# Which pieces of weights go through the fifth slot: new lists for mixers and FFNs of a two-block transformer forward pass

## What is computed

```
for l in range(2):                                   # first block
    x = x + 0.5 * swiglu(rmsnorm(x), w_ffn1_in[l], w_ffn1_out[l])      # 1024 -> 2*2816 -> 1024
    u = rmsnorm(x); parts = split(u @ w_in[l])
    y = mla_branch (8 heads, causal), hgrn2_branch (4 heads, gated recurrence, chunks of 64),
        memory_branch (4 heads over 256 memory tokens)
    x = x + (sum of sigmoid(gate_i) * (y_i @ w_o_i)) @ w_out[l]
    x = x + 0.5 * swiglu(rmsnorm(x), w_ffn2_in[l], w_ffn2_out[l])
x = rmsnorm(x)
for l in range(2):                                   # second block
    FFN, then x = x + concat(rwkv7_group, retnet_group) @ w_out_2[l], then FFN
return rmsnorm(x)
```

## Time and profile before

| | us |
|---|---|
| three runs | 2357.98, 2355.84, 2358.05; median 2357.98 |
| the profiled execution's own time | 2355.99 |
| its span, first to last instruction | 2354.2 |
| PE busy | 2333.3 (99%) |
| DVE busy | 1639.6 (70%) |
| ACT busy | 1277.4 (54%) |
| DMA queue q1 | 401.62 MB, 47.4% of 16 engines |

### The profile page before, as it was taken

How to read it: one execution, slowest core, us unless ns; L and a number is a source line. 1 busy time by engine, 2 the same in 40 slices (tenths; PEclk the granted TensorE clock), 3 DMA queues, 4 the chain that set the end, 5 groups by cost and what they waited for, 6 DMA issues and landing times.

```text
span 2354.2 us, 50733 instructions
## 1 busy us (share of the span) xinstructions
PE 2333.3 (99%) x21750; PEld 2275.3 (97%) x21750; DVE 1639.6 (70%) x2270; ACT 1277.4 (54%) x1828; POOL 346.9 (15%) x296
## 2 busy tenths in 40 slices
PE   9999999999999999999999999999999999999998
PEld 9999999999999999999999999989999999989998
DVE  7865777966677657878666766776765766776763
ACT  6644656654455456565455554636554554646554
POOL 2012020300200210203003002431002002431001
PEclk9999999999999999999999999999999999999999
DMA  6555533465555545335555645422655545422643
GB/s 255 202 193 194 179 126 126 180 213 182 197 194 190 192 180 185 118 141 183 197 196 181 223 180 197 168 80 91 215 180 197 197 182 196 173 74 92 216 180 124
DMA packets 57680, 410.21 MB, mean 174 GB/s; under 512 B 6384, under 2 KB 6640, under 8 KB 8688
## 3 DMA queue, kind: packets, MB, share of 16 engines
q1 hardware_dynamic: 56448, 401.62, 47.4%
q10 hardware_dynamic: 1008, 5.34, 0.6%
HBM read 405.89 MB, written 1.05 MB: 173 GB/s over the span
## 4 chain that ended last, share of the span: by engine, by line
PE 84%; DVE 7%; ACT 4%; issue 4%; POOL 1%; DMA 0%; DVEq 0%; ACTq 0%; SPq 0%; POOLq 0%
PE bank L558 83%; DVE sb_wlo L514 3%; DVE area L1862 1%; ACT sb_whi L506 1%; PE bank L2210 1%; ACT area L1582 0%; DVE area L1845 0%; DVE area L1811 0%; DVE area L648 0%; POOL sb_x_ssq L701 0%; ACT area L1648 0%; DVE area L1919 0%; ACT area L1606 0%; POOL area L839 0%; ACT area L1603 0%
## 5 line engine op out<-in xcount | busy, mean ns | idle before, releaser
L558 PE MATMUL bank<-area,sb_whi 128*128 128x256 f32 x11752 | 2017.1, 278 | 3.1 <-ACT area L782 1.2
L558 PEld LDWEIGHTS bank<-area,sb_whi 128*128 128x128 f32 x11752 | 1769.1, 188 | 12.6 <-issue 4.2
L558 PE MATMUL bank<-area,sb_wlo 128*128 128x256 f32 x5876 | 1606.4, 277 | 5.2 <-DVE sb_wlo L514 5.0
L506 ACT ACTIVATE sb_whi<-sb_raw 128x1024 fp32r<-128x1024 f32 x762 | 793.0, 1055 | 596.0 <-PE bank L558 582.6
L558 PEld LDWEIGHTS bank<-area,sb_wlo 128*128 128x128 f32 x5876 | 1094.4, 188 | 7.7 <-DVE sb_wlo L514 7.6
L514 DVE TENSOR_TENSOR sb_wlo<-sb_raw,sb_whi 128x1024 fp32r<-128x1024 f32 x762 | 954.7, 1264 | 156.8 <-ACT sb_whi L506 154.9
L648 DVE TENSOR_TENSOR area<-bank,sb_x_diag 128x512 f32<-128x512 f32 x244 | 166.8, 684 | 72.0 <-PE bank L558 49.7
L999 DVE TENSOR_TENSOR area<-area,area 128x256 f32<-128x256 f32 x176 | 76.2, 433 | 186.7 <-ACT area L950 185.5
L558 PE MATMUL bank<-area,area 64*64 64x64 f32 (+5 forms) x2864 | 149.5, 248 | 0.1
L558 PEld LDWEIGHTS bank<-area,area 64*64 64x64 f32 (+3 forms) x2864 | 127.3, 139 | 19.2 <-ACT area L1630 5.3
L693 POOL TENSOR_TENSOR sb_x_ssq<-sb_x 128x256 f32<-128x256 f32 x9 | 12.0, 1331 | 849.3 <-DVE sb_x L1043 839.1
(11 more groups left out here) (272 smaller groups left out, 1148.3 us busy)
## 6 DMA issues: line engine op xcount, KB each, us to landing
sb_raw<-stream SPq DMA_DIRECT2D x379, 1024.0 KB, 4.8
sb_raw<-stream SPq DMA_DIRECT2D x3, 512.0 KB, 7.2
area<-lora ACTq DMA_DIRECT2D x2, 768.0 KB, 6.1
area<-c ACTq DMA_DIRECT2D x1, 1504.0 KB, 7.5
sb_x<-x SPq DMA_DIRECT2D x4, 256.0 KB, 5.4
area<-mem ACTq DMA_DIRECT2D x1, 1024.0 KB, 8.5
out<-sb_x SPq DMA_DIRECT2D x4, 256.0 KB, 2.9
sb_raw<-stream ACTq DMA_DIRECT2D x1, 512.0 KB, 4.8
```

Of the source, the lines that this page charges most:

```text
L506: e.activation(k.hi[k.slot[p]], raw_piece(k, p), ACT.Copy).then_inc(*k.done("weights_hi", p))
L558: return e.matmul(out, lhsT, rhs, start=start, stop=stop, skip_group_check=True, tile_position=at)
```

## The change

Only the lists differ, and one rule: the same set of pieces used to be at least four apart and now need be only two apart.

```diff
-SEEDS_FIRST, SEEDS, SEEDS_LATE = (0, 4, 18, 40), (2, 23, 45), (0, 4, 25, 47)
-SEEDS_MIX1 = (2, 8, 12, 16, 20, 24, 30, 35, 39, 43, 47, 51, 55, 59, 63, 67, 75)
-SEEDS_MIX2 = (4, 8, 12, 16, 22, 26, 30)
+SEEDS_FIRST, SEEDS, SEEDS_LATE, SEEDS_TWO = (0, 4, 18, 40), (2, 23, 45), (0, 4, 25, 47), (2, 9, 23, 45)
+SEEDS_MIX1 = (2, 8, 24, 30, 33, 39, 41, 43, 45, 47, 49, 51, 53, 55, 59, 61, 63, 67, 75, 78)
+SEEDS_MIX2 = (4, 8, 12, 22, 28)
...
             if i == 0:
                 want = SEEDS_FIRST
+            elif phases[i - 1].endswith("norm"):
+                want = SEEDS_TWO
...
-    assert all(q - p >= SPLIT_SLOTS for p, q in zip(out, out[1:]))
+    assert all(q - p >= 2 for p, q in zip(out, out[1:]))
```

## The result

| | before | after |
|---|---|---|
| median of four runs, us | 2358.02 (2355.84 to 2358.13) | 2420.76 (2419.47 to 2424.45) |
| ratio, 95% interval | | 1.0272 (1.0259 to 1.0285) |
| span of the profiled execution | 2354.2 | 2418.1 |
| sum forecast, over the profiled execution | | +46.9 |
| measured, over the profiled execution | | +63.9 |

The kernel became slower by 62.7 us in the medians. The forecast of 2405.0 was 15.8 short; the range of 2378 to 2426 holds the result.

The account below looks back on a forecast made before the run. PE, busy 99%, seemed the bound, but ACT's splits waiting for PE's seeds would close a loop through ACT and DVE. Costs 50.6 less gains 3.7 make 46.9 over 2355.99, 2402.9; plus 2.0 for the median, 2405 us (range 2378 to 2426).

Parts of the forecast that it names:

- the ring: Attention: PE's seed, ACT's split, ACT's step, DVE's step, PE's next seed wait in a circle; 18.4 us a mixer.
- The tests I had named: Attention: 10 long ACT waits per mixer, seeds 10 to 12 us apart, PE idle before level products, about 25 us longer.
- eight links at the mean of four, 2.3: Attention: eight seeds per mixer each priced at the 2.3 us mean of four worked-out steps, 18.4 us.
- a granted clock of 1.00: Attention: PE's granted clock stays 1.00, 2.4 GHz; the forecast is wrong if it leaves that; no cost counted.
- Rival 4: Attention: PE's clock falls to half while it stands idle, 108 us more over both mixers, about 2510; chance 0.03.
- the end of the attention: Piece 129 waits for 127, delaying ACT's chain that PE needs at piece 130: 4.7 us a mixer.
- the waits of pieces 99 and 127: Piece 99 waits for 96 and 127 for 125: 1.1 us each, the middle of nothing to 2.3.
- The gains: Faster matmuls in B0f1 (1.4), first-block mixers (1.7) and second-block mixers (0.6): 3.7 us saved.
- the two rhythms: PE: the same matmul takes 117.8 ns or 113.3 ns; a seed turns slow into fast, buying 4.4 ns each.
- The first, a hidden wait: Attention: slack behind ACT's split hides the wait, leaving only 3.7 us saved, 2354; chance 0.05.
- The second: Attention: each step costs only as the cheapest of four, 0.7 us, giving 2375; chance 0.05 at its far end.
- third: Attention: each step costs as the dearest of four, 3.9 us, giving 2430; chance 0.05 at its far end.

Follow-up runs that it names:

- the last version: Changed kernel with 33 back to 35, 61 out, ACT's splits running to p + 3 in attention steps 0 to 10: 2352.42 us against 2355.81 for the kernel before.

## Why the prediction was right in sign and short in size

**The ring was right, and so was its arithmetic.** Each sum ran from the end of one seed to the end of the next. The end of a seed is where the next piece starts, or, where ACT waits for it, the start of ACT's split:

| from the end of piece | forecast, us | measured | before | cost |
|---|---|---|---|---|
| 109 to 111 | 12.3 | 12.29 | 8.46 | 3.8 |
| 111 to 113 | 10.7 | 10.63 | 8.53 | 2.1 |
| 117 to 119 | 11.6 | 11.59 | 9.28 | 2.3 |
| 119 to 121 | 10.1 | 10.15 | 8.81 | 1.3 |

ACT's timeline of the changed kernel has the ends of the pieces 113, 117 and 119 (those of 109 and 111 stand above, at 334.70 and 346.99):

```profile
357.62 1.06 ACT L508 ACTIVATE sb_whi<-sb_raw 128x1024 fp32r<-128x1024 f32 x1 [6.33 <-PE bank L560]
...
380.65 1.06 ACT L508 ACTIVATE sb_whi<-sb_raw 128x1024 fp32r<-128x1024 f32 x1 [7.09 <-PE bank L560]
...
392.24 1.06 ACT L508 ACTIVATE sb_whi<-sb_raw 128x1024 fp32r<-128x1024 f32 x1 [7.03 <-PE bank L560]
```

All four sums are within 0.1 us. That the ring is the cause is shown by the kernel with ACT three ahead: same seeds, nothing lost in the steps. The tests I had named were met: waits of 6 to 10 us on ACT, seeds 10 to 12 us apart, PE idle ahead of the level products for DVE.

**The step that failed first: eight links at the mean of four, 2.3.** The eight links of A0mix, with no fall of the clock among them, cost 3.6, 3.4, 3.8, 2.1, 2.8, 2.4, 2.3 and 1.3, in all 21.7 against 18.4. Two things are in this. The link from 119 to 121 I compared with the time between two starts of seeds before, 9.48, where from end to end it is 8.81: 1.3 and not 0.7. More of it lies in the four links that I did not work out: they cost 12.1 and were taken at 9.2. The first two alone cost 6.9. In the first, ACT has an instruction that no later link has:

```profile
312.37 1.28 ACT L1584 ACT_TABLE_LOAD   x1
```

It was in the trace before as well, at 304.60, beside PE's pieces; in the ring it stands between the split and the exponentials that DVE waits for. No run takes it out, so its share of the link is not measured. The links grow cheaper towards the end of the attention, and a sample with half of its links from there had too low a mean. This term was short by 3.3 a mixer, 6.6 in all.

**The step that failed most: a granted clock of 1.00.** I had written that the forecast is wrong if the clock in the attention leaves 1.00. It did. The stretches of the changed kernel, the first being A0mix's attention, the fourth A1mix's (columns as in the earlier trace rows):

```profile
308.46:439.10 130.64, 109.45 (x973) 97.32 (x971) 79.34 (x149) 60.39 (x114) 17.32 (x14) 1.00 0.27 97
440.20:447.00 6.80, 5.45 (x25) 5.45 (x26) 5.65 (x6) 6.77 (x10) 0.00 (x0) 0.50 0.40 154
948.79:952.20 3.41, 3.41 (x9) 2.64 (x10) 1.23 (x1) 1.91 (x3) 0.00 (x0) 0.50 0.02 5
971.00:1111.00 140.00, 117.50 (x1003) 105.45 (x1001) 82.94 (x156) 61.98 (x117) 17.05 (x14) 0.96 0.25 91
```

In A0mix the grant stays 1.00 through all ten steps and falls once, after the end, for 6.8 us. In A1mix it falls five times, at 948.8, 982.9, 1010.2, 1058.0 and 1112.6, to 0.50 or 1.2 GHz for 3.4 us each. Since both mixers run the same program, they price it: the links cost 25.0 in A1mix and 21.7 in A0mix, so three falls there cost 3.3 (0.3, 1.5 and 1.5), and with 1.5 at piece 313, 2.4 at 131 and 1.5 at 346 it makes 8.7 us. The largest pause of PE with a fall behind it reads in PE's timeline

```profile
441.55 0.80 PE L560 MATMUL bank<-area,sb_whi 128*128 128x256 f32 x2 [4.10 <-DVE area L650]
```

with 0.80 for two matmuls where the earlier trace rows has 0.50. Rival 4 had this mechanism at 0.03 and with the price of whole stretches, 108 us. It should have had a size in between: a fall here and there. Its argument against, that small matmuls break each pause, did not hold. The ring hides a fall only where PE waits for DVE right after it, as at 982.9. The Trainium skill (TensorE: Matmul & The Clock Gate, HAM oscillation) says that waits between groups of matmuls bring the clock down and that each comes at a price. The trace agrees with the kind, with six falls, but not with one for each wait. It was right to take this as a rival and wrong to give it one price only.

**The smaller terms.** For the end of the attention I carried 4.7; piece 130 lost 4.4. For the waits of pieces 99 and 127 I took 1.1 each out of 0 to 2.3; they lost 1.7 (at piece 97 / 312) and 1.4 (from piece 122 to 129). These three are together 7.5 a mixer and not 6.9, 1.2 more for both.

**The gains were right.** 3.7 forecast, 3.6 measured where they are alone. They rest on the two rhythms of the rows. The Trainium skill (TensorE: Matmul & The Clock Gate, Back-to-back issue gap) gives the one gap that the prediction used for a single pair of matmuls, and says itself that a stream with weight loads keeps another spacing; it ties neither to where the operands lie. With one rhythm these lists would have saved nothing. That seeds in the ring gain nothing was right too; where there is no ring (the last version against the list without close seeds) they bring 0.5 for four seeds in each mixer.

**The sum again:** 46.9 forecast; 6.6 for the links, 8.7 for the clock, 1.2 for the smaller terms and 0.1 for the gains make 63.5, and 0.4 is left over as shifts of some tenths at single pieces. That the range still holds the result is in part luck: its upper end came from dearer links, it had no term for the clock, and the 8.7 us happened to fit.

**The rivals.** The first, a hidden wait, fell: two links alone lost 8.5 us a mixer. The second and third, 0.7 and 3.9 a link, fell as well: the mean is 2.7. The fourth was partly true, as told.

## What to carry to other kernels

When a buffer is reused sooner, do not ask only whether the engine that refills it has time. Write down what stands behind the refill in its program, and follow it through the engines back to the use that frees the buffer: if the way closes, the loop's sum replaces the step's time, and busy shares (ACT 53% here) say nothing. Work out every step of such a loop and not a sample, and if PE gets pauses of a microsecond or more that it didn't have, put a few falls of its clock into the sum.

## What the runs showed of the hardware that I had not expected

- The granted clock fell for 3.4 us at a time (6.8 once), in a pause of PE of 0.8 to 4.1 us or within 2 us after one, where I had expected either none or a whole stretch. Not every such pause has a fall behind it: the 2.34 us before piece 97 had none in the changed kernel's A0mix and one in A1mix, where piece 312 comes after the same 2.34 us, and one in the kernel with number 33 alone. Of the ten such pauses in the five kernels with number 33, eight have one. Nor is their number the same in each execution of one kernel: of the changed kernel's four runs, the two of 2419.5 and 2419.9 us have a mean granted clock of 0.994, the longest, 2424.45, has 0.992. What decides it stays open.
- A fall of 3.4 us costs 1.4 to 1.5 us where PE is last (pieces 98, 313, 346), and as much in the ring when it comes on a seed's own matmuls (links 3, 5 and 7). It costs 0.3 in the first link, where PE goes on to wait for DVE.
- One piece less of lead, for ACT at the end of the attention, costs 1.3 us at piece 130 and 2.4 at piece 131 in each mixer, with either list. The lead of four is needed at that one place and not in the ten steps before.
